# A two-layer attention and short-convolution trunk: query tensor in one piece, reordered first steps, GpSimd low parts, a shorter stage end

## The reference, cut to what matters

```python
proj = h @ w_in                                   # h: 2064 tokens (16 meta + 2048) x 1024
c_q, c_kv, k_rope, z = split(proj, [384, 640, 672])
q = (rms_norm(c_q) @ w_uq)                        # 16 heads x (64 plain + 32 rotary)
q_rope = rope(q[..., 64:]); k_rope = rope(k_rope) # one rotary key for all heads
c_kv = rms_norm(c_kv); k_nope, v = c_kv @ w_uk, c_kv @ w_uv
s = (q_nope @ k_nope.T + q_rope @ k_rope.T) * scale    # masked by 64-token chunks
o = softmax(s) @ v
h = layer_norm(alpha * h + (o * silu(z)) @ w_o)
b, c, u, z = split(h @ conv_w_in, 4)              # layer 1: gated causal convolution, width 3
h = layer_norm(alpha * h + (b * conv(c * u) * silu(z)) @ conv_w_out)
```

## Time and profile before

| | us |
|---|---|
| median of 3 runs | 2818.47 (2814.31 to 2821.31) |
| profiled execution | 2829.5 |
| its span, first to last instruction | 2827.7 |
| mean granted TensorE clock | 0.975 |

### The profile page before, as it was taken

The page is one execution under the profiler, slowest core; times in us unless marked ns, Lnnn a source line. Parts: engine busy times, 40 slices in busy tenths (PEclk is TensorE's granted clock), DMA queues, the critical chain, the costliest instruction groups (busy, mean ns, idle before and its releaser), DMA issues. The chain is left out here.

```text
span 2827.7 us, 45472 instructions
## 1 busy us (share of the span) xinstructions
PE 2660.8 (94%) x16756; PEld 2434.5 (86%) x16756; DVE 1597.0 (56%) x3262; ACT 1219.4 (43%) x3055; POOL 752.2 (27%) x332
## 2 busy tenths in 40 slices
PE   5998899999999999999999979969999999999898
PEld 5898899999888989898989858859988899889686
DVE  5556571129888878898988848854112111121465
ACT  4333222238887878887878841112111001110211
POOL 0000000013344544433444204441211111211244
PEclk8999999999999999999999989989999999999999
DMA  4545344312243334333333335643111011110543
GB/s 139 187 152 170 123 140 137 106 45 47 49 92 82 87 77 90 80 73 69 78 70 70 62 106 166 190 157 105 37 45 37 22 37 37 37 31 17 175 154 113
DMA packets 235457, 260.88 MB, mean 92 GB/s; under 512 B 86992, under 2 KB 188240, under 8 KB 228880
## 3 DMA queue, kind: packets, MB, share of 16 engines
q1 hardware_dynamic: 217600, 250.11, 32.3%
q10 hardware_dynamic: 17680, 8.46, 1.1%
HBM read 165.77 MB, written 92.20 MB: 91 GB/s over the span
## 5 line engine op out<-in xcount | busy, mean ns | idle before, releaser
L1159 DVE TENSOR_TENSOR b_pt_lo<-b_transposed,b_pt_hi 128x384 fp32r<-128x384 f32 (+4 forms) x784 | 429.2, 564 | 50.9 <-ACT b_pt_hi L1062 46.1
L1052 ACT ACTIVATE arena<-b_ring,b_nmax 128x384 f32<-128x384 f32 (+7 forms) x784 | 435.6, 560 | 49.9 <-DVE b_nmax L1151 41.1
L43 PE MATMUL d_ring<-d_h_hi,d_w_hi 128*128 128x410 f32 (+1 forms) x1152 | 426.0, 370 | 17.4 <-POOL d_w_lo L1465 15.7
L1062 ACT ACTIVATE b_pt_hi<-b_transposed 128x384 fp32r<-128x384 f32 (+4 forms) x784 | 382.1, 501 | 128.0 <-PE b_transposed L1092 115.8
L44 PE MATMUL d_ring<-d_h_lo,d_w_hi 128*128 128x410 f32 (+1 forms) x1152 | 426.7, 370 | 0.0
L45 PE MATMUL d_ring<-d_h_hi,d_w_lo 128*128 128x410 f32 (+1 forms) x1152 | 425.5, 369 | 0.0
L1146 DVE TENSOR_REDUCE b_cmax<-b_ring 128x1 f32<-128x384 f32 (+4 forms) x736 | 396.1, 542 | 36.0 <-PE b_ring L45 22.0
L1092 PE MATMUL b_transposed<-identity,arena 128*128 128x128 f32 (+2 forms) x2448 | 383.0, 274 | 18.0 <-DVE b_pt_lo L1159 14.6
L1109 PE MATMUL b_o_ps<-b_pt_hi,b_v 128*128 128x256 f32 (+2 forms) x1280 | 335.7, 293 | 19.0 <-DVE arena L1165 18.3
L1092 PEld LDWEIGHTS b_transposed<-identity,arena 128*128 128x128 f32 (+2 forms) x2448 | 280.8, 135 | 69.6 <-issue 40.1
L1110 PE MATMUL b_o_ps<-b_pt_lo,b_v 128*128 128x256 f32 (+2 forms) x1280 | 314.3, 282 | 0.0
(11 more groups left out here) (165 smaller groups left out, 4882.9 us busy)
## 6 DMA issues: line engine op xcount, KB each, us to landing
arena<-x_a SPq DMA_DIRECT2D x23, 1032.0 KB, 5.5
d_w_st<-w_conv SPq DMA_DIRECT2D x32, 512.0 KB, 3.4
keys<-arena SPq DMA_DIRECT2D x64, 129.0 KB, 5.2
queries<-arena SPq DMA_DIRECT2D x64, 129.0 KB, 3.0
gates<-arena SPq DMA_DIRECT2D x64, 129.0 KB, 2.2
arena<-keys SPq DMA_DIRECT2D x16, 516.0 KB, 4.8
arena<-queries SPq DMA_DIRECT2D x16, 516.0 KB, 8.9
values<-arena SPq DMA_DIRECT2D x32, 256.0 KB, 2.2
```

What stands on the lines that cost most here:

```text
L43: nc.tensor.matmul(out, w_hi, x_hi, start=start, stop=False)
L1052: nc.scalar.activation(p[0:rows, n % PSLOTS, 0:w], banks[0:rows, n % RING, 0:w], ACT.Exp, bias=nmax[0:rows, tile % 8:tile % 8 + 1], accum_ ...
L1062: nc.scalar.activation(turned(pt_hi, g, u, nb)[:, :, tile_columns(u, j)], tb[:, n % 2, 0:nb, 0:rows], ACT.Copy).then_inc(pt_hi_done, 1)
L1159: nc.vector.tensor_tensor(lo, tb[:, n % 2, 0:nb, 0:rows], hi.bitcast(F32), ALU.subtract).then_inc(pt_split, 1)
```

## The change

Queries become one tensor of 16 heads x 128 rows (64 plain, 32 cosine, 32 sine), which a head's load reads in one DMA; the swap of the sine halves moves to the rotary keys, whose load takes one more DMA. Stage p's first steps: chunk 0's key is kept in `kt` by a plain copy, so that its bank is free; the sines and both rotations come after the second projection; the load of x chunk 2 stands before the value pieces. GpSimd makes the low part of pieces 1 to 29. In query steps `newton` comes after the second take. The last head's sums are inverted before the fifth last low part and stored before the last output, and stage b's final waits move into stage c's loads, whose semaphores now outlive stage b.

```diff
@@ load_queries (stage b and first head) is removed; FIRST_KEYS 96 -> 112
-    sp.dma_start(raw[0:64, :], qn_d[h // 2, 64 * (h % 2):64 * (h % 2) + 64, :]).then_inc(semaphore, 16)
-    sp.dma_start(raw[64:96, :], qc_d[h // 4, at:at + 32, :]).then_inc(semaphore, 16)
-    sp.dma_start(raw[96:112, :], qs_d[h // 4, at + 16:at + 32, :]).then_inc(semaphore, 16)
-    sp.dma_start(raw[112:P, :], qs_d[h // 4, at:at + 16, :]).then_inc(semaphore, 16)
@@ stage_p, SP: store
+                elif what == "q":
+                    to = q_d[2 * m:2 * m + 2, 0:64, chunk_cols(g)]
+                elif what == "r":
+                    to = q_d[4 * m:4 * m + 4, 64:96, chunk_cols(g)]
                 else:
-                    to = {"k": k_d, "q": queries[0], "r": queries[1], "z": z_d}[what][m, :, chunk_cols(g)]
+                    to = {"k": k_d, "z": z_d}[what][m, :, chunk_cols(g)]
                 sp.dma_start(to, stage_of(r, rows_of(r))).then_inc(stored[SLOT[r]], 16)
                 if what == "r":
-                    sp.dma_start(queries[2][m, :, chunk_cols(g)], sines_of(r)).then_inc(stored[SLOT[r] + 1], 16)
+                    sp.dma_start(q_d[4 * m:4 * m + 4, 96:P, chunk_cols(g)], sines_of(r)).then_inc(stored[SLOT[r] + 1], 16)
@@ stage_p, SP: first loads, key stores
-            for i in range(3, 7):
-                load_piece(i)
+            load_piece(3)
+            load_piece(4)
+            load_x(2)
+            load_piece(5)
+            load_piece(6)
...
-                    if g == 1:
-                        load_x(2)
-                    if g < NCA:
-                        sp.wait_ge(k_sum, g + 1)
-                        sp.dma_start(kr_d[:, chunk_cols(g)], krs[0:32, :]).then_inc(kr_out, 16)
+                    for c in {0: (), 1: (0, 1)}.get(g, (g,) if g < NCA else ()):
+                        sp.wait_ge(k_sum, c + 1)
+                        sp.dma_start(kr_d[:, chunk_cols(c)], krs[0:32, :]).then_inc(kr_out, 16)
@@ stage_p, SP: first head
-                    sp.dma_start(rot[96:P, :], kr_d).then_inc(first_in, 16)
+                    for half in range(2):
+                        sp.dma_start(rot[96 + 16 * half:112 + 16 * half, :], kr_d[16 - 16 * half:32 - 16 * half, :]).then_inc(first_in, 16)
...
-                    load_queries(sp, rot, 0, queries, first_in)
+                    sp.dma_start(rot[:, :], q_d[0]).then_inc(first_in, 16)
@@ stage_p, GpSimd
+            for i in range(len(PIECES)):
+                pool.wait_ge(w_hi_done, i + 1)
+                pool.wait_ge(w_split, i)
+                if i:
+                    nc.gpsimd.tensor_tensor(piece_to(i, 1), piece_raw(i), piece_to(i, 0).bitcast(F32), ALU.subtract).then_inc(w_split, 1)
@@ stage_p, ScalarE: after split_x(1)
+            copies(0)
+            split_weights(PIECES_AT["p", 0])
...
                     if g == 1:
                         root(0)
+                        split_x(2)
                         latent(0)
+                        copies(1)
+                        split_weights(PIECES_AT["p", 1])
+                        act.wait_ge(angle, 1)
+                        for half in range(2):
+                            for part in range(2):
+                                nc.scalar.activation(rot[...], ang[...], ACT.Sin).then_inc(sined, 1)
+                        shift_key(0)
+                        shift_key(1)
+                        continue
@@ stage_p, TensorE: bank_free
-                    pe.wait_ge(k_turned, g)
+                    pe.wait_ge(k_turned, 1 if g == 1 else g + 1)
@@ stage_p, VectorE
+            def keep_key():
+                dve.wait_ge(proj, 3)
+                nc.vector.tensor_copy(kt, banks[:, 2, 0:CA]).then_inc(k_turned, 1)
...
             split_half_x0(0)
-            split_weights([("x", 0)])
+            split_first_weights()
             split_half_x0(1)
-            split_weights([("x", 1)])
...
             split_x(1)
+            squares(0)
+            keep_key()
+            then(nc.vector.scalar_tensor_tensor(ang, turns, -TURN3, ang, ALU.mult, ALU.add))
...
                         normalise(0)
+                        split_x(2)
                         latent(0)
-                    if g != 1:
-                        split_weights(extra)
+                    else:
+                        split_x(g + 1)
                     squares(g)
+                    if g == 1:
+                        rotate_key(0)
                     if g < NCA:
                         rotate_key(g)
...
                     take(mine[0])
-                    split_weights(extra[0:2])
                     if chain:
                         inverse(g + 1)
+                    take(mine[1])
+                    if chain:
                         newton(g + 1)
-                    take(mine[1])
-                    split_weights(extra[2:])
-                    if chain:
                         normalise(g + 1)
@@ stage_b, SP
             def next_queries(h):
                 sp.wait_ge(k_split, h + 1)
-                load_queries(sp, raw, h + 1, queries, raw_in)
+                sp.dma_start(raw[:, :], q_d[h + 1]).then_inc(raw_in, 16)
...
+                    if h == HEADS - 1 and u == UNITS - 1:
+                        sums(h)
                     output(h * UNITS + u)
                     if u == 1 and h:
                         sums(h - 1)
-            sums(HEADS - 1)
-            sp.wait_ge(r_out, 32 * HEADS)
-            sp.wait_ge(gate_out, 16 * (2 * HEADS - 4))
-            sp.wait_ge(o_out[0], 16 * same_parity(HEADS * UNITS - 2))
-            sp.wait_ge(o_out[1], 16 * same_parity(HEADS * UNITS - 1))
@@ stage_b, VectorE
                 elif letter == "L":
+                    if n == len(TURNED) - SUMS_BEFORE:      # SUMS_BEFORE = 5
+                        inverse_sums(HEADS - 1)
...
-            inverse_sums(HEADS - 1)
@@ stage_c, SP: load(i)
+                if i == 0:
+                    sp.wait_ge(gate_out, 16 * (2 * HEADS - 4))
+                    sp.wait_ge(r_out, 32 * HEADS)
+                    sp.wait_ge(o_out[0], 16 * same_parity(HEADS * UNITS - 2))
+                    sp.wait_ge(o_out[1], 16 * same_parity(HEADS * UNITS - 3))
+                if i == NTC - 2:
+                    sp.wait_ge(o_out[1], 16 * same_parity(HEADS * UNITS - 1))
@@ program
-    queries = scratch("queries", [PAIRS, P, T]), scratch("cos_queries", [HEADS // 4, P, T]), scratch("sin_queries", [HEADS // 4, P, T])
+    q_d = scratch("queries", [HEADS, P, T])
```

More of the change, by code:

```diff
@@ L176, in stage_p @@
 def stage_p(nc, own, dram):
-    x_a, w_x, w_uk, w_uv, w_uq, pos, rope_c, gains, ident_d, k_d, kr_d, v_d, queries, z_d = dram
+    x_a, w_x, w_uk, w_uv, w_uq, pos, rope_c, gains, ident_d, k_d, kr_d, v_d, q_d, z_d = dram
     wx_hi, wx_lo, region, rot, stage = own.big_hi, own.big_lo, own.region, own.rot, own.stage
@@ L401, in _ @@
             split_x(1)
[L402 to L406 removed]
+            copies(0)
+            split_weights(PIECES_AT["p", 0])
             for kind, g in STEPS_P:
                 if kind == "p":
[L409 to L410 removed]
+                    if g == 0:
+                        continue
                     if g == 1:
                         root(0)
+                        split_x(2)
                         latent(0)
[L414 to L415 removed]
+                        copies(1)
[3 more added lines that the diff above has]
+                            for part in range(2):
+                                nc.scalar.activation(rot[64 * part:64 * part + 32, half * HALF_T:half * HALF_T + HALF_T],
+                                                     ang[64 * half + 32 * part:64 * half + 32 * part + 32, :], ACT.Sin).then_inc(sined, 1)
+                        shift_key(0)
+                        shift_key(1)
+                        continue
+                    split_x(g + 1)
+                    split_weights(PIECES_AT.get((kind, g), ()))
                     copies(g)
[L417 to L418 removed]
+                    shift_key(g)
                 else:
@@ L640, in _ @@
             for kind, g in STEPS_P:
-                extra = list(PIECES_AT.get((kind, g), ()))
                 if kind == "p":
-                    if g:
-                        split_x(g + 1)
+                    if g == 0:
+                        continue
                     if g == 1:
@@ L711, in _, with own_memory @@
                     latent(g + 1)
-                for n, r in enumerate(mine[first + 4:]):
+                for r in mine[first + 4:]:
                     take(r)
-                    split_weights(extra[3 + n:4 + n])
 PSLOTS = 14
-Own = namedtuple("Own", "region big_hi big_lo rot work small w_raw x_raw stage raw_v o_b o_t p ident stored")
-def own_memory(nc, ctx, ident, big_hi, big_lo):
+Own = namedtuple("Own", "region big_hi big_lo rot work small w_raw x_raw stage raw_v o_b o_t p ident stored o_out r_out gate_out")
+def own_memory(nc, ctx, outer, ident, big_hi, big_lo):
     sb = lambda n, s, d=F32: ctx.enter_context(nc.sbuf_tensor(n, s, d))
```

(18 more changed lines are left out.)

57 lines of the change are left out of this document (21 added, 36 removed).

## The result

The kernel after takes 2908.12 us (median of 4 runs, 2905.89 to 2912.77), the kernel before 2819.81 (4 runs beside it). The ratio is 1.0319, interval 1.0299 to 1.0339: slower by 88 us. The forecast was 2927, 2880 to 2980. The profiled execution has a span of 2911.0 us, 83.3 more than before.

What follows compares the result with a forecast made beforehand. TensorE bounds the kernel, and two store queues bind the query steps. 120 (query stores) - 3 + 5 (start, o2 and o3) - 6 (query loads) - 7 (stage ends) = +109 on 2818.5: 2927 us, range 2880 to 2980.

Steps and rivals of the forecast that it cites:

- The bound: Whole kernel: TensorE busy 2660.8 of 2827.7 us, so other engines count only where it waits or its clock falls.
- Query stores: Projections' second half: stores run on 2 and 4 engines, 49 ns a row, steps 40.9 us for 24.7: +120 us.
- the ring of 8 slots: Staging in query steps: holds 384 rows, 18.8 us of store work that may still run when the stage's last step ends.
- Query loads: Attention: one DMA for four lets values and output store go 1.5 us sooner: -6 us, bounds 0 and -18.
- A gain of 0.5 us each: Attention: what each wait for an output store was taken to gain from one-DMA query loads, -6 us in all.
- Start, and steps o2 and o3: Projections' first steps: earlier second projection, -3 us; GpSimd pieces between newton's small products in o2 and o3, +5 us.
- Steps o8 to o15: Query steps: some 20 us of stalls and half-clock stretches freed, but the stores bind there: 0.
- rival 1: Query steps: stores spread over 16 engines all the same, so stalls are freed: -31, 2788 us; chance 0.15.
- Stage end: End of attention: last head's sums issued 6.6 us sooner, next stage's loads follow: -7 us, bounds -5 and -8.
- Rival 2: Stores on 16 engines, and GpSimd blocks VectorE more than counted: 0, 2819 us; chance 0.03.
- Rival 3: Query steps: store queue starved between steps, fed 9/10 of the time: 153 for 120, 2960 us; chance 0.82 together with the forecast.

Runs made afterwards that it cites:

- The undo: Changed kernel with the three query tensors, stores and four-DMA loads of before: 0.9902; or with each query store split into 2 DMAs: 0.9855.
- the part alone: Kernel before with only the one query tensor (its stores, one-transfer loads, rope keys in one DMA more): 1.0356, 2902.81 us.
- the dose: Changed kernel with only cosine and sine stores split in four (576 rows): 1.0087; with only query stores split in two (320 rows): 0.9855.
- the kernel with three tensors: Changed kernel with the three query tensors of before, stores of 128 rows and four-DMA loads, all else of the change kept: 0.9902, 2776.06 us.
- the one with split query stores: Changed kernel with each query store as 2 DMAs of 64 rows, cosine and sine stores left as one DMA: 0.9855, 2769.45 us.
- the GpSimd kernel: Kernel before with GpSimd making the low parts of pieces 1 to 29 and nothing else changed: 1.0006, 2815.01 us.

## Why the prediction was right

**The bound.** Right: TensorE's steps became longer only where something else made it wait, and that carried the forecast.

**Query stores.** The mechanism is the one forecast, in each of its steps. Completions are 2 and 4; a step lasts 40.3 to 42.8 us after the first (forecast 40.9); first to last store 323.0 us (318); ScalarE and VectorE wait in `take` for query stores; the DMA share falls from 0.46 to 0.29, over a third and not the forecast half. The undo removes it (1.0319 to 0.9902 or 0.9855), the part alone brings it (1.0356), and the dose gives 32 us at 576 rows, 41 at 768, and 23 at 320, where TensorE binds. The trace of before couldn't decide between 16 engines and 2 and 4, as the prediction says, so that choice was argued and not measured; the runs bear it out. The rule of the Trainium skill ("DMA: Bandwidth & Descriptors", section "Why a DMA increments its semaphore by 16 and not by 1") holds here in both halves: 2 and 4 completions for outer counts of 2 and 4, and both kinds on the same engines. The one landing that was to show it (10 us or more for a store) has no row: the view gives no landing time for such a store. The waits of up to 9.7 us in `take` and the 9.5 us from the last issue to ScalarE's last wait stand in for it.

The size is 112 and not 120. The price of a row was right: the steps without weight pieces lasted 40.3 to 40.9 us, for a forecast of 40.9 at 49 ns a row. From the first query store to ScalarE's last wait for one, it is 332.5 us (235.76 to 568.25), where the forecast had 337. And the next chunk got 22.6 us ahead beside the queue's last rows (332.5 - 197.6 - 112.3), where the forecast took back 19 for the ring of 8 slots. Besides the slots TensorE has four banks: ScalarE takes the first gate block at 553.28, 5.5 us before the last query store's issue, which before came 1.4 us ahead of it. That the forecast for first to last store (318 us) is near the measured 323.0 is in part luck, since it took the 19 us off there: at the last issue only 9.5 us of stores were left, as the issues themselves were held back. These readings are from the traces and weren't tried by themselves.

**Query loads.** The step that was mis-sized: -20 measured for -6. "A gain of 0.5 us each" was reckoned from "the same bytes stand ahead of that store". The bytes are the same, but the output store's issue comes 3.9 us sooner (medians 5.2 and 1.3 us after the first query load) and not 1.5, since SP is held at single issues on the way, and the values land 1.3 us sooner. VectorE's wait for output stores, 11 to 13 times a run, loses nearly all of itself (20.9 to 2.5 us). The measured gain, 18 us between the means of the later traces (1026.1 and 1008.1), is at the bound of -18 that the forecast had set and not chosen.

**Start, and steps o2 and o3.** Right to 2 us: +0.1 for +2, the sum of a gain and a loss that were both forecast. The second projection at 21.9 (19.4 to 24.6), key block 4 at 53.1 (47.4 or 55.0), the stall in o2 3.17 us (3.4). The two parts cancel: GpSimd's alone costs 7.7 us by the first query store, and the reordering gives as much back. VectorE's small instructions beside GpSimd's pieces took 2.38 and 2.58 us in place of 0.30 and 0.43, each until GpSimd's product had ended, as another product did in the earlier trace rows. By the section "Who interferes with whom" of the Trainium skill's "SBUF — State Buffer" the blocked ones are those with two SBUF inputs or in a mode that uses both ports. The second of the two (L601) has two inputs and agrees; the first (L600) has one, so by that rule it would be in such a mode, which no row here shows.

**Steps o8 to o15.** The forecast put 20 us of stalls down as freed but hidden behind the stores: so it was. With the stores mended they appear: 176.6 us from first to last store in place of 197.0. They come mostly from newton's place (14.6 us by itself) and less from the low parts. That is why rival 1, 2788 us, was a good forecast for the wrong condition: the kernel with three tensors measured 0.9902 (2792 us at 2819.8), the one with split query stores 0.9855 (2779).

**Stage end.** -7.7 in the trace, 5.6 by itself: forecast -7, -5 to -8. Right.

**Added up from the kernels that did one part each:** +100 (tensor, with its faster loads), +1.7 (GpSimd), -8 or so (reordered start, the difference between 243.0 and 233.3 to 235.8 for the first query store), -5.6 (stage end), and newton's -14.6 hidden behind the stores: +88. Measured +88.3. That it fits so closely is luck: the GpSimd kernel's +1.7 holds 5.8 us gained in query steps, which the stores hide too, so +94 would be the fairer sum, and the terms are uncertain by 2 to 5 us each.

**The rivals.** Rival 2 (16 engines, and GpSimd blocks VectorE more) isn't seen: the engines are 2 and 4, and the low parts alone give 1.0006. Rival 3 (a starved queue, 153 us) neither; the first step of the second half (37 us) was shorter, and none was above 43.

## What to carry to other kernels

Before a store or load gets an outer dimension of 2 or 4, count its completions. Here it ran on 2 or 4 engines, both kinds on the same ones, and every row then waited in one queue. Lay the scratch tensor out so that the rows of a block keep one uniform stride (alternating rows do), or split the transfer and count the issues. A gain for the reader of a tensor has to be set against what its writer pays, and a part whose gain is hidden should be tried without what hides it: here the other parts were worth 28 us together (0.9902), and that could not be seen under one that cost 100.

## What the runs showed of the hardware that was not expected

Issues of stores of 32 and 64 rows cost SP 0.56 us on average in a row of 18 (0.42 for most of 32 rows, 0.60 for most of 64), no less than one of 128 rows before (0.33 in the earlier trace rows, 0.45 behind another), so 49 of them fill 27.5 us, and splitting stores further makes the issues the bound. Where the lone engines' queues were long, an issue itself took longer: 3.07 us for a query store in the kernel after, 1.46 for an x load (437.46) and 1.54 for a sine store (558.76), where a store took 0.33 before. So SP's time is full in such a step although it issues no more than before, and whatever stands behind the stores in its order comes late. The same is seen in attention, where the output store's issue is held behind four query loads and hardly behind one. And two chips differed by some 15 us in attention alone, with the same kernel, where the stages around it agreed within 2 us.
